# Latent attention of a two-layer trunk: scores with the keys on the partitions, the softmax shift as a 97th row, sums by GpSimd

## The reference

```python
def mla_block(q_nope, q_pe, k_nope, k_pe, v):
    scale = (C_NOPE + C_ROPE) ** -0.5
    s = (jnp.einsum('bhqd,bhkd->bhqk', q_nope, k_nope)
         + jnp.einsum('bhqr,bkr->bhqk', q_pe, k_pe)).astype(jnp.float32) * scale
    p = jax.nn.softmax(s, axis=-1)
    return jnp.einsum('bhqk,bhkd->bhqd', p.astype(v.dtype), v)
```

## Time and profile before

| what | value |
|---|---|
| median of 3 runs | 3637.82 us |
| the profiled execution: its own time, its span | 3635.24 us, 3633.4 us |
| granted TensorE clock over the span | 0.956 |
| PE, PEld, DVE, ACT, POOL busy over the span | 91%, 76%, 51%, 32%, 8% |
| the stage of latent attention | 2214 to 2755 us |

### The profile page before, as it was taken

One profiled execution on the slowest core, in us unless ns is written; L12 is line 12 of the kernel. 1 busy time (PEld: TensorE's weight loads), 2 busy tenths in 40 slices (PEclk: granted clock), 3 DMA queues, 4 the chain that ended last, 5 costly groups with the idle time before them and its releaser, 6 DMA issues. The chain is left out here.

```text
span 3633.4 us, 47627 instructions
## 1 busy us (share of the span) xinstructions
PE 3315.9 (91%) x18952; PEld 2778.4 (76%) x18952; DVE 1837.9 (51%) x2088; ACT 1169.5 (32%) x1913; POOL 279.8 (8%) x525
## 2 busy tenths in 40 slices
PE   3999599797999999999979698999999799999998
PEld 1787477686788888888868587888887588888886
DVE  4599666454344444444453334555555444444446
ACT  2112155466211111111146323555553312111121
POOL 1000000111000000000012111111111100000001
PEclk6999799898999999999989799999999899999999
DMA  4322587332211111111042743322212221111113
GB/s 182 85 81 102 160 271 247 115 117 65 59 47 46 35 35 35 35 38 42 31 138 82 275 158 89 106 56 44 60 40 82 64 64 46 52 46 58 35 46 116
DMA packets 277081, 316.29 MB, mean 87 GB/s; under 512 B 83824, under 2 KB 222672, under 8 KB 275904
## 3 DMA queue, kind: packets, MB, share of 16 engines
q1 hardware_dynamic: 264160, 267.09, 24.6%
q0 software_dynamic: 12768, 47.08, 3.4%
HBM read 243.54 MB, written 70.58 MB: 86 GB/s over the span
## 5 line engine op out<-in xcount | busy, mean ns | idle before, releaser
L1103 DVE TENSOR_TENSOR y_sum<-ffn_down_ps,y_sum 128x512 f32<-128x512 f32 x396 | 271.3, 690 | 235.3 <-PE ffn_down_ps L90 233.4
L88 PE MATMUL ffn_gate_ps<-y_hi,ffn_w_hi 128*128 128x512 f32 (+1 forms) x880 | 326.2, 371 | 37.4 <-DVE ffn_w_lo L1059 37.4
L88 PE MATMUL ffn_down_ps<-ffn_w_hi,ffn_act_hi 128*128 128x512 f32 x792 | 312.5, 395 | 16.8 <-DVE y_sum L1103 10.4
L89 PE MATMUL ffn_gate_ps<-y_lo,ffn_w_hi 128*128 128x512 f32 (+1 forms) x880 | 325.7, 370 | 0.0
L90 PE MATMUL ffn_gate_ps<-y_hi,ffn_w_lo 128*128 128x512 f32 (+1 forms) x880 | 325.4, 370 | 0.0
L89 PE MATMUL ffn_val_ps<-y_lo,ffn_w_hi 128*128 128x512 f32 (+1 forms) x880 | 323.9, 368 | 0.0
L88 PE MATMUL ffn_val_ps<-y_hi,ffn_w_hi 128*128 128x512 f32 (+1 forms) x880 | 323.8, 368 | 0.0
L90 PE MATMUL ffn_val_ps<-y_hi,ffn_w_lo 128*128 128x512 f32 (+1 forms) x880 | 323.7, 368 | 0.0
L89 PE MATMUL ffn_down_ps<-ffn_w_lo,ffn_act_hi 128*128 128x512 f32 x792 | 309.3, 391 | 0.0
L90 PE MATMUL ffn_down_ps<-ffn_w_hi,ffn_act_lo 128*128 128x512 f32 x792 | 308.8, 390 | 0.0
L1059 DVE TENSOR_TENSOR ffn_w_lo<-ffn_raw,ffn_w_hi 128x1024 fp32r<-128x1024 f32 x132 | 158.0, 1224 | 282.0 <-ACT ffn_w_hi L1014 282.0
(11 more groups left out here) (293 smaller groups left out, 7017.3 us busy)
## 6 DMA issues: line engine op xcount, KB each, us to landing
ffn_raw<-in_ffn_w_up SPq DMA_DIRECT2D x88, 512.0 KB, 3.8
da_ada_w<-in_ada_w SPq DMA_DIRECT2D x10, 4096.0 KB, 24.9
ffn_raw<-in_ffn_w_down SPq DMA_DIRECT2D x44, 512.0 KB, 5.7
ab_raw<-in_ab_w_in SPq DMA_DIRECT2D x20, 512.0 KB, 3.8
mod_ada_w<-in_ada_w SPq DMA_DIRECT2D x4, 2048.0 KB, 11.4
scratch_mla_q_hi<-up_out_hi POOLq DMA_DIRECT2D x12, 512.0 KB, 2.9
scratch_mla_q_lo<-up_out_lo POOLq DMA_DIRECT2D x12, 512.0 KB, 3.2
scratch_qk_hi<-ab_qk_hi POOLq DMA_DIRECT2D x8, 640.0 KB, 3.2
```

The costliest lines, as they stand in the source:

```text
L88: pe.matmul(out, a_hi, b_hi, start=first, stop=False)
L89: pe.matmul(out, a_hi, b_lo, start=False, stop=False)
L1103: dve.tensor_tensor(part, down_ps[:, half, :], part, ALU.add).then_inc(s.sum_done, 1)
```

## The change

The stage is rewritten with the **keys on the partitions** from the start. A step is now one tile of 128 keys (`kt`, ten to a head) against all 1024 queries, in two halves of 512 columns.

- **Rough pass.** A softmax needs a shift per query before the exponential, and with the keys on the partitions a row maximum cannot be taken. So the scores of each head are also made in the old layout from the rounded parts alone (`rough`, one matmul per chunk instead of three), VectorE takes their negated maximum, and two times four transposes (`shift`) turn the 1024 maxima into a row, which ScalarE writes as row 97 of `q_hi`. Row 97 of `k_hi` is all ones, so the first score matmul adds the shift. The rough pass of head `h+1` runs during head `h`, one unit in eight of its ten steps; that of head 0 runs ahead of everything.
- **No transposes of exponentials.** `pt` comes out of the exponential directly in the layout the product needs, and the PSUM copies fall away.
- **Sums.** GpSimd adds the ten tiles of a head (nine adds of 128x1024), and one float32 matmul per half with a 128x64 matrix of ones sums over the partitions and spreads the result. VectorE inverts it in two pieces of 128x256 and scales the output in two pieces of 64x512. ScalarE and VectorE, no longer GpSimd, split the output, 128x1024 once per two heads.

The core of the diff:

```diff
         def _(sp):
             def head(h):
                 if h >= 2:
-                    sp.wait_ge(s.s_full.sem, (h - 1) * XT)
+                    sp.wait_ge(s.s_full.sem, (h - 1) * KT * HALVES)
                 load_head(sp, h, qs[h % 2], ks[h % 2], q_parts, k_parts, qk_in[h % 2].sem)
...
+            def rough(h, u):
+
+                if h >= C_HEADS:
+                    return
+                q_hi, k_hi = qs[h % 2][0], ks[h % 2][0]
+                if u == 0 and h == 0:
+                    pe.wait_ge(first_in, 16 * FIRST_LOADS)
+                elif u == 0:
+                    pe.wait_ge(qk_in[h % 2].sem, 16 * QK_LOADS * ((h + 1) // 2))
...
+                if h:
+                    pe.wait_ge(s.max.sem, h * UNITS + u)
+                elif u >= 2:
+                    pe.wait_ge(s.max.sem, u - 1)
+                out = rough_bank(h, u)
+                for a, width in chunks:
+                    mm = pe.matmul(out[:, a:a + width], q_hi[0:HD, u * P:(u + 1) * P], k_hi[0:HD, a:a + width],
+                                   start=True, stop=True)
+                mm.then_inc(s.rough_full.sem, 1)
...
+            def scores(h, kt, half):
...
+                if kt == 0:
+                    pe.wait_ge(s.shifted.sem, h * HALVES + half + 1)
...
+                if n >= 2:
+                    pe.wait_ge(s.exp.sem, n - 1)
+                out, keys, tokens = s_bank(half), slice(kt * P, (kt + 1) * P), slice(half * BANK, (half + 1) * BANK)
+                pe.matmul(out, k_hi[0:HD + 1, keys], q_hi[0:HD + 1, tokens], start=True, stop=False)
+                pe.matmul(out, k_hi[0:HD, keys], q_lo[0:HD, tokens], start=False, stop=False)
+                pe.matmul(out, k_lo[0:HD, keys], q_hi[0:HD, tokens], start=False, stop=True).then_inc(s.s_full.sem, 1)
...
+            def sums(h):
+
+                pe.wait_ge(s.added.sem, (h + 1) * ADDS)
...
+            for u in range(UNITS):
+                rough(0, u)
+                if u == HALF_UNITS + 1:
+                    shift(0, 0)
+            shift(0, 1)
+            for h in range(C_HEADS):
                 for kt in range(KT):
...
+                    for half in range(HALVES):
+                        scores(h, kt, half)
+                    if k:
+                        product(k - 1)
+                    if kt in ROUGH:
+                        rough(h + 1, ROUGH.index(kt))
+                    if kt == SUM and h:
+                        sums(h - 1)
+                    if kt in SHIFT:
+                        shift(h + 1, SHIFT.index(kt))
+            product(C_HEADS * KT - 1)
+            sums(C_HEADS - 1)
```

More of the change, by code:

```diff
@@ L2715, in latent_attention @@
     KT = TT
-    UNITS = C_HEADS * XT
-    PAIRS = UNITS // 2
-    PER_HEAD = XT // 2
-    chunks = token_chunks(T)
[L2720 to L2744, removed]
+    UNITS = XT
+    HALVES = SEQ // BANK
+    HALF_UNITS = UNITS // HALVES
+    SLOTS = 4
+    ADDS = KT - 1
+    ROUGH = (0, 1, 3, 4, 5, 6, 7, 8)
+    SUM = 2
+    SHIFT = (6, 9)
+    SPLIT = 7
+    INVERSES = 2
+    chunks = token_chunks(T)
     with ExitStack() as ctx:
@@ L2819, in bank_free @@
[L2819 to L2847, removed]
@@ new lines, in sums @@
+            def sums(h):
+                pe.wait_ge(s.added.sem, (h + 1) * ADDS)
+                pe.wait_ge(s.shifted.sem, min(h + 2, C_HEADS) * HALVES)
+                if h:
+                    pe.wait_ge(s.inverted.sem, h * INVERSES)
+                for half in range(HALVES):
+                    mm = pe.matmul(small_ps[half * C_V:(half + 1) * C_V, :], ones[:, :],
+                                   total[:, h % 2, half * BANK:(half + 1) * BANK], start=True, stop=True)
+                mm.then_inc(s.sums_full.sem, 1)
@@ L2922, in _ @@
+            for half in range(HALVES):
+                shift_copy(0, half)
+            for h in range(C_HEADS):
+                for kt in range(KT):
+                    for half in range(HALVES):
+                        exponential(h * KT + kt, half)
+                    if kt in SHIFT:
+                        shift_copy(h + 1, SHIFT.index(kt))
+                    if kt == SPLIT and h and h % 2 == 0:
+                        rounded(h // 2 - 1)
+            rounded(C_HEADS // 2 - 1)
         @block.vector
@@ new lines, in rest @@
+            def rest(g):
+                dve.wait_ge(s.y_rounded.sem, g + 1)
+                dve.tensor_tensor(y_lo[:, g, :], o_t[:, g % 2, :], y_hi[:, g, :].bitcast(F32), ALU.subtract)\
+                   .then_inc(s.y_done.sem, 1)
+            dve.memset(neg_max[:, 0, :, :], 0.0).then_inc(s.zeroed.sem, 1)
+            dve.memset(neg_max[:, 1, :, :], 0.0).then_inc(s.zeroed.sem, 1)
+            dve.wait_ge(s.zeroed.sem, 2)
+            for u in range(UNITS):
+                maximum(0, u)
+            for h in range(C_HEADS):
+                for kt in range(KT):
+                    if kt in ROUGH:
+                        maximum(h + 1, ROUGH.index(kt))
+                    if h and SUM <= kt < SUM + INVERSES:
+                        inverse(h - 1, kt - SUM)
+                    elif h and SUM + INVERSES <= kt < SUM + INVERSES + HALVES:
+                        output(h - 1, kt - SUM - INVERSES)
+                    if kt == KT - 1 and h and h % 2 == 0:
+                        rest(h // 2 - 1)
@@ new lines, in _ @@
+            for n, cell in enumerate(cells):
+                if n:
+                    pool.wait_ge(s.ones_set.sem, n)
+                pool.memset(cell, 1.0).then_inc(s.ones_set.sem, 1)
+            pool.wait_ge(s.ones_set.sem, ONES)
+            for h in range(C_HEADS):
+                for kt in range(1, KT):
+                    k = h * KT + kt
+                    pool.wait_ge(s.exp.sem, (k + 1) * HALVES)
+                    if kt == 1 and h >= 2:
+                        pool.wait_ge(s.sums_full.sem, h - 1)
+                    if h * ADDS + kt - 1:
+                        pool.wait_ge(s.added.sem, h * ADDS + kt - 1)
+                    first = pt[:, (k - 1) % SLOTS, :] if kt == 1 else total[:, h % 2, :]
+                    pool.tensor_tensor(total[:, h % 2, :], first, pt[:, k % SLOTS, :], ALU.add)\
+                        .then_inc(s.added.sem, 1)
```

251 lines of the change are left out of this document (96 added, 155 removed).

## The result

| | before | after |
|---|---|---|
| median | 3637.6 us (3637.31 to 3640.85) | 3751.03 us (3749.11 to 3751.25) |
| profiled execution: time, span | 3635.24, 3633.4 us | 3751.07, 3749.0 us |
| granted TensorE clock over the span | 0.956 | 0.939 |
| the stage, first matmul to last split | 2214.00 to 2755.11 | 2215.18 to 2869.97 |

Ratio 1.031, 95% interval 1.0295 to 1.0324: slower by 113 us, forecast was 3712 us, 74 slower. Nearly the whole difference lies in the stage, which lasts 654.8 us instead of 541.1: the next stage's first matmul starts at 2873.19 instead of 2758.33, 114.9 us later, and only 1.2 us of that lie ahead of the stage's first matmul.

A forecast was written before the change was run, and what follows sets the result against it. TensorE's instructions were taken to bound the stage. Start 42.6, fourteen heads 534, head 15 25.6 and tail 13 made 615 us against 541, +74, so 3712 us; likeliest case 3690 to 3742, with rivals 3680 to 3758.

The forecast's parts named there:

- the likeliest case: Load's wait and half clock behind it both happen: 3712 us, own range 3690 to 3742, chance 0.72.
- the wide one: The range of the likeliest case with the rivals beside it: 3680 to 3758 us.
- the prediction's own signs of being wrong: Rough matmuls start at once, or wait for a maximum instead of a DMA, or dense stretches exceed 30.7 us a head.
- The wait that the change adds: TensorE's first rough matmul waits for the next head's six DMAs: 5.1 us in 14 heads, 71 us.
- The clock behind the wait: After each load wait TensorE's clock is at half for 4.5 us, 2.25 lost, 14 times: 31 us; bounds none and 42.
- TensorE's work of a head: TensorE's scores, products, rough pass, shift and sums: 30.7 us a head against 33.2, a gain of 2.5.
- the rival "the gain stands": The load is no wait and TensorE's shorter work counts: 3610 us, faster by 28; chance 0.06.
- Start and end: Head 0's last score at 42.6 us, head 15 25.6 us, the tail behind its last score 13 us.
- The other engines: In 30.7 us a head: ScalarE 13 us, GpSimd's nine adds 22 us, VectorE's inverse 2.3 us each; none binding.
- The rivals on these three: VectorE's inverses bind at 4.4 us each, 3764 us, or GpSimd's adds from 3.4 us, about the same; chance 0.08.
- that of the halves in turn: The product's two halves run in turn on TensorE: 0.87 us more in 161 steps, +140, 3852 us; chance 0.03.
- The rival without the half clock: The load's wait comes but no half clock behind it: 3681 us; chance 0.10.

The follow-up runs named there:

- e1: The changed kernel without the loads of heads from 2 on and TensorE's wait for them, computing on old data: 3638.53 us, ratio 1.0006.
- e7: The changed kernel with the edits of e6 and e3 together, later rough pass and its three transfers first: 3642.72 us, ratio 1.0015.
- e2: The changed kernel with twenty overwritten matmuls of 512 columns ahead of TensorE's wait for the load: 3714.81 us, ratio 1.022.
- e6: The changed kernel with the rough pass two steps later and at the start of its step, loads untouched: 3695.49 us, ratio 1.0157.
- e3: The changed kernel with the rough pass's three transfers issued first under their own semaphore, scores waiting for the other three: 3665.7 us, ratio 1.0088.
- e5: The changed kernel with the products of two steps made together at every second step: 3754.57 us, ratio 1.0319.

## Why the prediction was right, and where it was short

The direction and the mechanism were right: 14 waits for the load, and a half clock behind each. The size was not. The measured 3751 us lie above the likeliest case's own range (3690 to 3742). They are inside the wide one (3680 to 3758) only through room that was given to rivals that did not happen, and so by luck. One of the prediction's own signs of being wrong came true: the dense work is 32.7 us a head, longer than 30.7.

- **The wait that the change adds.** Forecast 14 x 5.1 = 71 us, measured 14 waits and 72.8; load 9.2 us for 9.0. e1 shows that the loads carry the whole loss, e7 that it is the waiting and the clock behind it, not the transfers themselves.
- **The clock behind the wait.** Forecast 4.5 us at half, 31 us; measured 6.0 in the mean, 42 us by the records and 36 to 38 by e2. The mechanism was right, the size was within its stated bounds but not the one I took.
- **TensorE's work of a head.** This is the term that was mis-sized most: a step's product between scores was put at 1.05 us (bounds 0.87 and 1.92, 0.96 to 1.1 for the range). It takes 1.21 (1.67 less two starts of 0.23), 1.6 us more in ten steps. With the rest the head is 1.9 us longer, 14 x 1.9 = 26 us. I had read the change from the next start on either side, and had not looked one instruction further; its last row has a trace of it, two transposes in 0.44 us behind the product where two take 0.39 elsewhere. Of the forecast gain of 2.5 us a head against 33.2 only 0.5 is left. That is also why the rival "the gain stands" would have been wrong without any wait: e1 and e7 are at 3638 to 3643, not at 3610.
- **Start and end.** Head 0's last score was forecast 42.6 us behind the stage's first matmul and came 46.0 behind it (2261.14 against 2215.18). Up to the first score the sum was good, 14.9 us for 15.4. Behind it 1.3 us are the longer products (8 x 0.16), and some 2.7 are the clock, which was still at half when the scores began and for 5.5 us more:

```profile
2230.23:2235.76 5.53, 5.53 (x15) 4.34 (x15) 1.49 (x1) 3.49 (x5) 0.00 (x0) 0.52 0.00 0
```

- Head 15 took 27.6 us (forecast 25.6; 1.6 of the 2.0 are again the products), the tail from 2858.13 to 2869.97, 11.8 (forecast 13).
- **The whole.** 46.0 + 569.4 + 27.6 + 11.8 = 655 against 615 forecast: 26 for the dense work of 14 heads, 7 for the clock and 2 for the wait in them, 3.4 at the start, 2 in head 15, less 1 in the tail, together the 40 that were missing.
- **The other engines.** Add 2.41 us (taken 2.4), exponential 0.60 (0.6), inverse 1.75 (taken 2.3, bounds 0.42 to 4.4). The 2.1 us that the prediction estimated for it from the Trainium skill ("VectorE: DVE Perf Modes", First, the fixed hardware budget) were too high as well. TensorE waited for a maximum 2.9 us and for an add 1.2 in the stage. The rivals on these three fall; so does that of the halves in turn, since the two products of a step take 1.01 us to the next start (2366.86 to 2367.87).
- The rival without the half clock is e2's case, and came to 3715 instead of 3681: 26 of the 34 us are the dense work of the heads, the rest mainly the start, head 15 and the wait.

## What to carry to other kernels

When a change reads a double buffer earlier, subtract from the load's full length (first issue to last landing) only the work that stands between the last reader and the new reader; here some 4 of 9.2 us, and the idle rest cost half as much again in clock. When matmuls of another width and type stand between others, take their price from the starts of four neighbouring instructions, two on either side, and multiply it by how often they come. When the bottleneck engine's work gets shorter, look for the chain that is next before adding up the gain: here a maximum's 2.43 us and then an exponential took it.

## What the runs showed that was not expected

- The products of a step (plain float32, 64 columns, two side by side) between float32r matmuls of full width cost 0.35 us beyond their two rounds of 0.43, spread over three starts. Whether the width or the type costs it isn't separated.
- Behind waits of 4.7 to 6.3 us the half clock lasted 3.4 to 8.0 us; behind waits of 2.1 to 2.5 us (e6) it came in 8 heads and not in 4; in e3, with waits of 1.1 to 3.0 us, it came in two heads of 14, behind 1.6 and 3.0 us.
- An inverse of 128x256 takes 1749 ns where one of 128x2 takes 165. An estimate from the two is 6.2 ns a column and some 150 ns fixed; neither of my two bounds was near.
- Where a rough unit had to wait for the maximum in e5, it followed the one before into the same bank by 2.43 us, 0.94 more than the maximum itself takes (1.49).
